# Product-key experts without gathers: every expert streamed through matmuls, half of the tokens at a time

## The chip, the cores and the metric

The kernel runs on one core of a Trainium2 chip. The metric is the device time of one execution in microseconds (us), as the median of several runs. Beside it stands a profiled execution, taken by the hardware profiler, in which every instruction has its start and its duration; all rows below come from that one execution of the kernel before. The engines are TensorE (PE, with its weight loads as PEld), VectorE (DVE), ScalarE (ACT), GpSimd (POOL) and the sync engine (SP), which here issues DMAs only. Sixteen DMA engines move the data between the HBM and the on-chip memory. Everything is float32.

## The reference

Two decoder layers over 512 tokens of 1024 numbers. Each layer is a mixer (retention, dilated attention and mLSTM heads over one input projection, then an output projection and a layer norm, giving x1), and then two things are added to x1: the PEER experts and a gated embedding.

```python
def peer(x, wq, sub_keys, expert_u, expert_v):          # T = 512 tokens, D = 1024
    qry = (xf @ wq).reshape(T, 8, 2, 128)               # 8 heads, two halves of a query
    sc = einsum('thpc,hpnc->thpn', qry, sub_keys)       # 128 keys in each half
    s1, i1 = top_k(sc[:, :, 0], 16); s2, i2 = top_k(sc[:, :, 1], 16)
    cand = s1[..., :, None] + s2[..., None, :]          # 16 x 16 sums a head
    cidx = i1[..., :, None] * 128 + i2[..., None, :]
    top_s, sel = top_k(cand, 16)                        # 16 experts of 16384 a head
    g = softmax(top_s)
    a = gelu(einsum('td,tkd->tk', xb, expert_u[ib]))    # 128 experts a token
    return einsum('tk,tkd->td', a * gb, expert_v[ib])

x1 = layer_norm(DN_ALPHA * x + mix, ln1_g, ln1_b)
e = sigmoid(x1 @ ple_wg + ple_bg) * (p @ ple_wp)
x = layer_norm(DN_ALPHA * x1 + y + e, ln2_g, ln2_b)
```

The expert matrices U and V are 16384 x 1024 each per layer, 64 MB each. A token needs 128 rows of each.

## The kernel before

The order of the work is written out by hand in one program for each engine; engines meet at semaphores. A list of steps (`MIXER_STEPS`, line 70) sets the order of TensorE in the mixer. Its last entries are the output projection in 8 steps of 16 TensorE instructions each (`out`, L1547), the transposes of x1, and the first queries and scores.

The tokens lie in four blocks of 128, one token to a partition. The unit of the expert stage is a pair n of a block and a head, 32 pairs a layer (`PAIRS`), 16 experts each. For each of these 16:

- GpSimd issues two gathers (`gather_u`, L558, and `gather_v`, L567). Each brings one row of 4 KB for each of the 128 tokens, by row numbers that VectorE has written in `rows`. There are 8 slots for U rows and 8 for V rows.
- VectorE multiplies the 128 U rows with the tokens and sums along the row (`dot_products`, L1066), one instruction of 128x1024.
- After 16 of them ScalarE applies gelu (L607), VectorE weighs the results with the softmaxed gates (L1091), and ScalarE writes 16 diagonal matrices with these weights (L795).
- TensorE multiplies each diagonal with the V rows of its expert, in two halves of 512 columns (L1610), and accumulates in two PSUM banks over the whole block. In the second half of the first block and at the end some V rows are added by VectorE instead (`add_row`, 32 rows a layer).

The selection of the experts for later pairs (top 16 of each half, of the 256 sums, and the row numbers; `halves_step` and `pairs_step`, L946 to L1055) is cut into small steps between the dot products of VectorE. Queries (`query`, L1416) and scores (`score`, L1431, L1437) for the first block run at the end of the mixer, and for the other three blocks during the first pairs, the gated embeddings (`embedding`, L1571 to L1575) in pairs 16 to 24. A block's second layer norm (`layer_norm`, L849 to L861) follows when its last rows are added. SP loads weights: w_in and w_out for the mixer, then for each head 1 MB of wq, and the embedding's weights in two halves.

In the mixer the lines that the prediction uses are: L842, VectorE's tensor_scalar of the head norms, with two scalars read from a column; L1209, the first tap of the convolution; L544, L548 and L551, GpSimd's products; L1389, the input projection (256 columns wide for `att_v`).

The inner loop of TensorE in the expert stage is this:

```python
for k in range(TOPK):
    e.wait_ge(v_in[i % VR], ...)
    if k % (2 * VD) == 0:
        e.wait_ge(diag_ready, tensor_rows(i + 2 * VD))
    for m in range(2):
        ins = e.matmul(bank[m][:, :], diag[:, k, :], vrow[i % VR][:, m * 512:(m + 1) * 512], ...)
    ins.then_inc(v_free, 1)
```

## Time and profile before

| what | value |
|---|---|
| median of 3 runs | 3440.74 us (3437.34 to 3442.32) |
| span of the profiled execution | 3781.1 us |
| TensorE busy | 3004.2 us, 79% |
| VectorE busy | 2120.8 us, 56% |
| GpSimd busy | 1984.4 us, 52% |
| ScalarE busy | 676.8 us, 18% |
| moved by DMA | 1174.41 MB, 311 GB/s over the span |
| of it gathers | 1073.87 MB |

The profiled execution is 9% longer than the median of the runs without a profiler. A matmul instruction's duration holds the time in which it runs through the array beside the next one, so the sum of durations says more than the engine's work; the distance between two starts (the pitch) is the price of one in a dense row of them.

### The profile page before, as it was taken

The page shows a single profiled execution, that of the slowest core. Times are in us where ns is not written, and L with a number is a line of the kernel's source. Part 1 is how long each engine was busy: PE and PEld are TensorE (multiplying, and loading weights), DVE is VectorE, ACT ScalarE, POOL GpSimd, SP SyncE. Part 2 cuts the span into 40 slices and gives each one's busy share as a digit, 9 for nine tenths or more (in the row PEclk, how much of TensorE's full clock was granted, in tenths as well). Part 3 has the DMA queues.
Part 4 walks back from the last instruction along what each step waited for, and adds up shares of the span by engine and source line. Part 5 has one row for each costly group of instructions (what it writes and reads, how often), then busy time and mean ns, then how long its engine had stood idle before and what let it go on. Part 6 is the DMA issues. An engine that isn't in the chain of part 4 may idle for free.

```text
span 3781.1 us, 25835 instructions
## 1 busy us (share of the span) xinstructions
PE 3004.2 (79%) x7696; PEld 1341.3 (35%) x7696; DVE 2120.8 (56%) x4948; ACT 676.8 (18%) x1658; POOL 1984.4 (52%) x2100
## 2 busy tenths in 40 slices
PE   8999777778778888777699987777777788887776
PEld 4555433333223323222245544333322233333222
DVE  1447665575555655665424476665656555656654
ACT  1331111111111112111013211111111111121110
POOL 0014455566665666666500145555566666666665
PEclk9999888889999999999999998888899999999999
DMA  4127899998999999999831278998899999989998
GB/s 153 67 70 256 313 342 344 346 350 338 399 368 351 355 384 355 348 371 367 336 129 67 70 269 316 353 347 339 335 363 407 363 352 363 385 329 362 371 370 321
DMA packets 360799, 1174.41 MB, mean 311 GB/s; under 512 B 36946, under 2 KB 75986, under 8 KB 360404
## 3 DMA queue, kind: packets, MB, share of 16 engines
q0 software_dynamic: 294912, 1073.87, 74.7%
q1 hardware_dynamic: 63284, 98.59, 7.6%
q8 instruction: 61, 1.00, 0.1%
q10 hardware_dynamic: 2464, 0.31, 0.1%
q14 instruction: 78, 0.64, 0.0%
HBM read 1170.54 MB, written 2.10 MB: 310 GB/s over the span
## 4 chain that ended last, share of the span: by engine, by line
PE 27%; DVE 18%; POOL 16%; issue 15%; another core or an unknown queue 11%; DMA 9%; ACT 4%; DVEq 1%; ACTq 0%; SPq 0%; POOLq 0%
DVE arena L1066 10%; POOL arena L567 9%; PE bank L1610 8%; POOL arena L558 8%; DMA arena<-in_peer_v,rows 5%; PE bank L1389 5%; DMA arena<-in_peer_u,rows 4%; PE yv L1389 3%; ACT arena L795 3%; PE bank L1416 2%; PE yv L1547 1%; PE bank L1437 1%; PE yv L1467 1%; PE bank L1547 1%
## 5 line engine op out<-in xcount | busy, mean ns | idle before, releaser
L1610 PE MATMUL bank<-arena 128*128 128x512 f32 x3840 | 1906.7, 637 | 523.0 <-DMA arena<-in_peer_v,rows 318.4
L1066 DVE CUSTOM_DVE_ANT_0 arena<-arena,xps 128x1024 f32<-128x1024 f32 x1024 | 1237.4, 1214 | 629.3 <-DMA arena<-in_peer_u,rows 464.2
L567 POOL DMA_INDIRECT arena<-in_peer_v,rows x1024 | 974.6, 952 | 714.1 <-issue 281.8
L1610 PEld LDWEIGHTS bank<-arena 128*128 128x128 f32 x3840 | 719.3, 200 | 1696.4 <-issue 938.4
L558 POOL DMA_INDIRECT arena<-in_peer_u,rows x1024 | 972.5, 950 | 552.1 <-issue 293.0
L607 ACT ACTIVATE arena<-arena 128x16 f32<-128x16 f32 x64 | 13.9, 218 | 1897.9 <-issue 1160.9
L795 ACT ACTIVATE arena<-keep,arena 128x128 f32<-128x128 f32 x960 | 294.2, 388 | 299.1 <-remote 147.8
L1416 PE MATMUL bank<-xT,arena 128*128 128x128 f32 (+1 forms) x1024 | 250.2, 399 | 57.4 <-issue 55.5
L1416 PEld LDWEIGHTS bank<-xT,arena 128*128 128x128 f32 x1024 | 165.3, 203 | 132.5 <-issue 72.3
L1389 PE MATMUL bank<-arena,xT 128*128 128x512 f32 (+1 forms) x448 | 187.1, 573 | 6.4 <-DMA arena<-in_w_in 4.3
L1389 PE MATMUL yv<-arena,xT 128*128 128x512 f32 (+1 forms) x320 | 132.6, 569 | 0.0
L1437 PE MATMUL bank<-arena 128*128 128x128 f32 x192 | 46.9, 434 | 100.5 <-ACTq L628 90.8
L1339 DVE TENSOR_TENSOR arena<-arena,bank 128x512 f32<-128x512 f32 x16 | 11.0, 687 | 195.3 <-ACTq L806 118.1
L1389 PEld LDWEIGHTS bank<-arena,xT 128*128 128x128 f32 x448 | 84.9, 193 | 99.8 <-issue 90.7
L1571 PE MATMUL bank<-arena,xT 128*128 128x512 f32 x256 | 112.5, 592 | 0.0
L544 POOL TENSOR_TENSOR arena<-arena,normg 128x256 f32<-128x256 f32 x8 | 5.8, 726 | 189.7 <-ACTq L719 189.7
L1437 PEld LDWEIGHTS bank<-arena 128*128 128x128 f32 x192 | 42.2, 329 | 119.2 <-ACTq L628 106.0
L1066 DVE DVE_READ_ACCUMULATOR2_ANT arena<- 128x1 f32 x1024 | 84.1, 82 | 0.0
L1389 PEld LDWEIGHTS yv<-arena,xT 128*128 128x128 f32 x320 | 60.9, 195 | 62.1 <-issue 60.5
L540 POOL MEMSET arena<- 128x3 f32 x8 | 0.4, 101 | 142.5 <-PE xps L1485 142.5
L1571 PEld LDWEIGHTS bank<-arena,xT 128*128 128x128 f32 x256 | 48.6, 190 | 61.2 <-issue 61.2
L1547 PE MATMUL yv<-arena,xT 128*128 128x512 f32 x160 | 69.7, 592 | 0.0
(288 smaller groups left out, 1966.1 us busy)
## 6 DMA issues: line engine op xcount, KB each, us to landing
arena<-in_peer_wq SPq DMA_DIRECT2D x32, 1024.0 KB
arena<-in_w_in SPq DMA_DIRECT2D x12, 2048.0 KB, 8.0
arena<-in_peer_u,rows POOLq DMA_INDIRECT x1024
arena<-in_peer_v,rows POOLq DMA_INDIRECT x1024
arena<-in_w_out SPq DMA_DIRECT2D x4, 2048.0 KB, 8.2
arena<-in_ple_wg SPq DMA_DIRECT2D x4, 2048.0 KB
arena<-in_mixer SPq DMA_DIRECT2D x2, 2112.0 KB, 19.4
ln<-in_ln SPq DMA_DIRECT2D x8, 512.0 KB, 7.9
```

The source lines that it names most:

```text
L558: e.indirect_dma_start(urow[i % UR], None, a["peer_u"], bass.IndirectOffsetOnAxis(ap=rows[:, n % RR, k:k + 1], axis=0)).then_inc(u_in[i % ...
L567: e.indirect_dma_start(vrow[i % VR], None, a["peer_v"], bass.IndirectOffsetOnAxis(ap=rows[:, n % RR, k:k + 1], axis=0)).then_inc(v_in[i % ...
L607: e.activation(act_d, dots[:, n % 2, :], ACT.Gelu).then_inc(gelu_done, 1)
L795: e.activation(diag[:, k, :], ident, ACT.Copy, scale=wgt[:, n % 2, k:k + 1]).then_inc(diag_ready, 1)
L1066: e.tensor_tensor_reduce(r, r, xps[:, :], 1.0, 0.0, ALU.mult, ALU.add, dots[:, n % 2, k:k + 1]).then_inc(u_free, 1)
L1389: ins = e.matmul(ps[:, 0:w], xT[:, k, i * P:(i + 1) * P], wt[:, k, :], start=(k == 0), stop=(k == KT - 1))
L1416: ins = e.matmul(ps[:, at:at + hi - lo], wq[m % 2][:, k, n * P:(n + 1) * P], xT[:, k, lo:hi], start=(k == 0), stop=(k == KT - 1))
L1437: ins = e.matmul(ps[:, b * NKEYS:(b + 1) * NKEYS], qT[:, s, b * P:(b + 1) * P], keys[m % KR][:, s, :], start=True, stop=True)
L1467: ins = e.matmul(ps[:, :], wt[:, k, i * P:(i + 1) * P], xT[:, k, :], start=(k == 0), stop=(k == KT - 1))
L1547: ins = e.matmul(ps[:, :], xT[:, k, b * P:(b + 1) * P], wt[:, k % 4, side * 512:(side + 1) * 512], start=(k == 0), stop=(k == KT - 1))
L1571: e.matmul(ps[:, :], xT[:, k, b * P:(b + 1) * P], wg[:, k, :], start=(k == 0), stop=False)
L1610: ins = e.matmul(bank[m][:, :], diag[:, k, :], vrow[i % VR][:, m * 512:(m + 1) * 512], start=(h == 0 and k == 0), stop=(h == PH - 1 and k ...
```

## The change

The gathers go. In their place each of the 16384 experts is applied to each token, and the gates, which are zero for all but the 128 chosen experts of a token, leave the others out.

- The tokens are taken in two passes of 256 (`PASSES`, `PB` = 2 blocks). In each pass 128 tiles of 128 experts are read in order, U and V, by SP.
- U tiles come in four DMAs, each into 32 partitions, laid so that VectorE's transpose of 32x32 blocks over 128x1024 (`turn`) leaves a quarter of the 1024 inputs in each group of 32 partitions. x1 is rearranged to the same order by GpSimd before its transposes, and wq and ple_wg are loaded in quarters.
- `dots`: 8 matmul calls of 256 columns for a tile give 128 experts x 256 tokens. ScalarE applies gelu (`gelu`), VectorE multiplies with the gates of the tile (`weigh`), and `mix_rows` multiplies with the V tile: 4 calls of 512 columns, accumulated in PSUM over the 128 tiles of the pass. TensorE does the dots of tile n + 2 before the rows of tile n.
- The gates of a pass are a map of 128 x 128 expert numbers x 256 tokens (`gate`). A token's map is one matmul of 128x128: a one-hot matrix of the second halves' numbers (128 choices x 128) times one of the first halves' with the gate as its value. The two are written by `make_hot`, on GpSimd for the first 40 tokens and every third, otherwise on VectorE, in a ring of 4 slots. ScalarE copies four maps at a time (`copy_gates`).
- The whole selection of the first two blocks is made before the first tile, that of the other two blocks in steps between the tiles of pass 0. The maps of the second pass are made between the passes.
- Queries of both halves and all gated embeddings come before the first tile. The sum of alpha times x1 and the embedding is built in `x` by GpSimd and kept in the HBM while `x` holds the scores of the second half.

The diff, cut to its core:

```diff
+TILES = EXPERTS // P
+PASSES = 2
+PB = NB // PASSES
+PT = PB * P
+RING = 3
+AHEAD = 2
+UR, TR, VR, QR = 2, 2, 3, 4
+GROUP = 4
+HOT = GROUP
+DQ, DP = 4, 32
...
-    + [("out", 0), ("out", 1), ("out", 2), ("x1_tr", 0), ("q", (0, 0)), ("s", (0, 0)), ("q", (1, 0)), ("s", (1, 0)),
-       ("out", 3), ("out", 4), ("out", 5), ("out", 6), ("out", 7),
-       ("q", (2, 0)), ("s", (2, 0)), ("q", (3, 0)), ("s", (3, 0))]
+    + [("out", 0), ("out", 1), ("out", 2), ("out", 3), ("x1_tr", 0), ("out", 4), ("out", 5), ("x1_tr", 1),
+       ("out", 6), ("out", 7), ("q", (0, 0)), ("q", (1, 0)), ("s", (0, 0)), ("x1_tr", 2), ("q", (2, 0)), ("s", (1, 0)),
+       ("q", (3, 0)), ("s", (2, 0)), ("x1_tr", 3), ("q", (4, 0)), ("s", (3, 0)), ("q", (5, 0)), ("s", (4, 0)),
+       ("q", (6, 0)), ("s", (5, 0)), ("q", (7, 0)), ("s", (6, 0)), ("s", (7, 0))]
...
+GATE_STEPS = (
+    [("ple", u) for u in range(2 * NB)]
+    + [("q", (0, 1)), ("q", (1, 1)), ("s", (0, 1)), ("q", (2, 1)), ("s", (1, 1)), ("exp", 0)]
+    + [t for h in range(3, PH) for t in (("q", (h, 1)), ("s", (h - 1, 1)))] + [("s", (PH - 1, 1)), ("sel", 0)]
+    + spreads(0, 0, 10) + [("exp", 1)] + spreads(0, 10, GROUPS_A_BLOCK) + [("sel", 1)] + spreads(1, 0, GROUPS_A_BLOCK)
+)
+NEXT_STEPS = [t for b in range(PB, NB) for t in [("sel", b)] + spreads(b, 0, GROUPS_A_BLOCK)]
...
+def on_pool(b, t):
+
+    return b == 0 and t < 40 or t % 3 == 2
...
+        def make_hot(e, b, t):
+
+            e.wait_ge(selT_ready, b + 1)
+            n = b * P + t
+            if n >= HOT:
+                e.wait_ge(*hot_consumed(*TOKENS[n - HOT]))
+            h = hot[:, n % HOT]
+            e.tensor_scalar(h[:, 1, :], iota, selT[:, 1, t:t + 1], None, ALU.is_equal)
+            e.tensor_scalar(h[:, 0, :], iota, selT[:, 0, t:t + 1], selT[:, 2, t:t + 1], ALU.is_equal, ALU.mult).then_inc(hot_made(b, t)[0], 1)
...
+                def load_u(n):
+                    if n >= UR:
+                        e.wait_ge(u_turned, n - UR + 1)
+                    at = (l * TILES + n % TILES) * P
+                    src = a["peer_u"][at:at + P, :].rearrange("(g e) (q d) -> q e g d", g=DQ, q=DQ)
+                    for q in range(DQ):
+                        dst = utile[n % UR][q * DP:(q + 1) * DP, :].rearrange("p (g d) -> p g d", g=DQ)
+                        e.dma_start(dst, src[q]).then_inc(u_in[n % UR], 16)
+                def load_v(n):
+                    if n >= VR:
+                        e.wait_ge(v_used, n - VR + 1)
+                    e.dma_start(vtile[n % VR], a["peer_v"][(l * TILES + n % TILES) * P:(l * TILES + n % TILES + 1) * P, :]).then_inc(v_in[n % VR], 16)
+                for n in range(PASSES * TILES):
...
+                    load_u(n + AHEAD + UR + 1)
+                    load_v(n + VR)
...
+                def copy_gates(b, n):
+                    t = (b % PB) * P + n * GROUP
+                    if b >= PB:
+                        e.wait_ge(w_ready, (b // PB) * TILES)
+                    src = work_read(e, "spread", (b, n)).rearrange("p (t e) -> p e t", t=GROUP)
+                    e.copy(gate[:, :, t:t + GROUP], src).then_inc(work_freed("spread", (b, n)), 1)
+                def gelu(n):
+                    e.wait_ge(dots_full, n + 1)
+                    if n >= RING:
+                        e.wait_ge(v_used, n - RING + 1)
+                    e.activation(ring[:, n % RING, :], bank[n % 2][:, 0:PT], ACT.Gelu).then_inc(gelu_done, 1)
...
+                def turn(n):
+                    if n < PASSES * TILES:
+                        e.wait_ge(u_in[n % UR], DQ * 16 * (n // UR + 1))
+                        if n >= TR:
+                            e.wait_ge(dots_full, n - TR + 1)
+                        e.transpose(turned[n % TR].rearrange("p k g e -> p g k e"), utile[n % UR].rearrange("p (g k c) -> p g k c", g=DQ, k=KT)).then_inc(u_turned, 1)
+                def weigh(n):
+                    p, j = divmod(n, TILES)
+                    if j == 0:
+                        e.wait_ge(gate_written, p + 1)
+                    e.wait_ge(gelu_done, n + 1)
+                    r = ring[:, n % RING, :]
+                    e.tensor_tensor(r, r, gate[:, j, :], ALU.mult).then_inc(w_ready, 1)
...
+                def spread(b, n):
+                    ps = work_fill(e, "spread", (b, n))
+                    for i in range(GROUP):
+                        t = n * GROUP + i
+                        e.wait_ge(*hot_made(b, t))
+                        h = hot[:, (b * P + t) % HOT]
+                        ins = e.matmul(ps[:, i * P:(i + 1) * P], h[:, 1, :], h[:, 0, :], start=True, stop=True)
+                        ins.then_inc(work_filled("spread", (b, n)) if i == GROUP - 1 else hot_used, 1)
+                def dots(n):
+                    p = n // TILES
+                    e.wait_ge(u_turned, n + 1)
+                    if n >= 2:
+                        e.wait_ge(gelu_done, n - 1)
+                    u = turned[n % TR].rearrange("p k g e -> p k (g e)")
+                    for k in range(KT):
+                        ins = e.matmul(bank[n % 2][:, 0:PT], u[:, k], xT[:, k, p * PT:(p + 1) * PT], start=(k == 0), stop=(k == KT - 1))
+                    ins.then_inc(dots_full, 1)
+                def mix_rows(n):
+                    p, j = divmod(n, TILES)
+                    e.wait_ge(v_in[n % VR], 16 * (n // VR + 1))
+                    e.wait_ge(w_ready, n + 1)
+                    for b in range(PB):
+                        for m in range(2):
+                            ins = e.matmul((yv, xps)[b][:, m * 512:(m + 1) * 512], ring[:, n % RING, b * P:(b + 1) * P], vtile[n % VR][:, m * 512:(m + 1) * 512], start=(j == 0), stop=(j == TILES - 1))
+                    ins.then_inc(v_used, 1)
...
+                for n in range(AHEAD):
+                    dots(n)
+                for n in range(PASSES * TILES):
+                    if n == TILES:
+                        for step, i in NEXT_STEPS:
...
+                    if n + AHEAD < PASSES * TILES:
+                        dots(n + AHEAD)
+                    mix_rows(n)
```

## Rows read from the trace of the kernel before

**Rows 1.** The page: span, busy time, the gathers' queue (packets, MB, share).

```profile
span 3781.1 us, 25835 instructions
PE 3004.2 (79%) x7696; PEld 1341.3 (35%) x7696; DVE 2120.8 (56%) x4948; ACT 676.8 (18%) x1658; POOL 1984.4 (52%) x2100
q0 software_dynamic: 294912, 1073.87, 74.7%
```

**Rows 2.** Windows: stretch, its length, busy us of each engine, clock, DMA share, GB/s.

```profile
1500.00:1800.00 300.00, 220.54 (x449) 82.24 (x448) 182.89 (x398) 54.80 (x143) 199.09 (x208) 0.95 0.95 359
```

**Rows 3.** Timeline of TensorE at 1200 us: start, length, instruction, idle before and releaser.

```profile
1201.85 1.98 PE L1610 MATMUL bank<-arena 128*128 128x512 f32 x4 [0.58 <-DMA arena<-in_peer_v,rows]
1204.41 1.98 PE L1610 MATMUL bank<-arena 128*128 128x512 f32 x4 [0.58 <-DMA arena<-in_peer_v,rows]
```

**Rows 4.** Groups of instructions by line: busy us, mean ns, idle before.

```profile
L1610 PE MATMUL bank<-arena 128*128 128x512 f32 x3840 | 1906.7, 637 | 523.0 <-DMA arena<-in_peer_v,rows 318.4 <-issue 134.7 <-ACT arena L795 59.2
```

**Rows 5.** Timeline of TensorE, dense stretches of 256, 128 and 512 columns.

```profile
134.47 3.62 PE L1389 MATMUL bank<-arena,xT 128*128 128x256 f32 x16
304.89 3.74 PE L1416 MATMUL bank<-xT,arena 128*128 128x128 f32 x32
309.73 13.90 PE L1547 MATMUL yv<-arena,xT 128*128 128x512 f32 x32
323.46 13.90 PE L1547 MATMUL bank<-arena,xT 128*128 128x512 f32 x32
```

**Rows 6.** Windows as in the second group, and a piece of the chain (start, length).

```profile
353.00:358.00 5.00, 4.81 (x33) 4.62 (x31) 3.20 (x6) 1.96 (x4) 4.09 (x4) 0.75 1.05 386
362.00:391.60 29.60, 29.41 (x66) 13.03 (x67) 25.38 (x67) 5.84 (x16) 15.18 (x15) 0.94 0.94 345
362.19 29.40 PE bank L1610 x64
```

**Rows 7.** Timeline, one line's durations (min/median/max ns), GpSimd's groups.

```profile
134.50 4.19 DVE L842 TENSOR_SCALAR acc<-acc,mv,rstd 128x128 f32<-128x128 f32 x16
L842 DVE TENSOR_SCALAR acc<-acc,mv,rstd x64: 302/336/1276, 134.5 to 2151.9; 128x128 f32<-128x128 f32 x32, 128x64 f32<-128x64 f32 x32
269.32 1.32 POOL L548 TENSOR_TENSOR arena<-arena,normg 128x512 f32<-128x512 f32 x1 [8.66 <-ACTq L730]
270.79 1.26 POOL L551 TENSOR_TENSOR acc<-acc,arena 128x512 f32<-128x512 f32 x1
L544 POOL TENSOR_TENSOR arena<-arena,normg 128x256 f32<-128x256 f32 x8 | 5.8, 726 | 189.7 <-ACTq L719 189.7
```

**Rows 8.** Groups that price VectorE's and ScalarE's new work: busy us, mean ns.

```profile
L1209 DVE TENSOR_SCALAR arena<-arena,convw 128x512 f32<-128x512 f32 x8 | 3.9, 486 | 27.6 <-ACTq L698 27.6
L1143 DVE TENSOR_TENSOR arena<-bank,arena 128x256 f32<-128x256 f32 x12 | 4.5, 414 | 0.0
L987 DVE FIND_INDEX8 topi<-arena 128x8 uint32<-128x128 f32 x28 | 8.0, 285 | 0.0
L1026 DVE FIND_INDEX8 pos<-arena 128x8 uint32<-128x256 f32 x28 | 11.7, 419 | 0.0
L1040 DVE TENSOR_TENSOR arena<-arena,keep 128x1024 f32<-128x1024 f32 x28 | 34.4, 1227 | 3.2 <-remote 2.2
L778 ACT COPY xT<-bank 128x512 f32<-128x512 f32 x12 | 7.0, 586 | 2.8 <-PE bank L1584 2.7
```

**Rows 9.** Timeline and chain: first out step, end of layer 0, output.

```profile
277.60 7.03 PE L1547 MATMUL bank<-arena,xT 128*128 128x512 f32 x16
1884.30 1.28 DVE L1327 TENSOR_TENSOR acc<-acc,bank 128x512 f32<-128x512 f32 x2
1890.79 9.05 DMA arena<-in_w_in
2165.94 13.73 PE yv L1547 x32
3774.14 0.39 SPq L520 DMA_DIRECT2D out<-x  x1
```

927 lines of the change are left out of this document (354 added, 573 removed).

## The prediction

> **What bounds the kernel now.** I read the page first: TensorE is busy 79% of the span, and the software queue of the gathers moves 1073.87 MB and takes 74.7% of the 16 DMA engines' time over the span, mixers included [rows 1]. A busy share names no bound, so I took one late window and the timeline inside the gather stage. In 1500 to 1800 us the DMA engines are 95% busy at 359 GB/s, TensorE 220.54 of 300 us, VectorE 182.89 [rows 2]. The timeline shows four TensorE instructions of 1.98 us and then 0.58 us of waiting for a V row set, again and again, every 2.56 us [rows 3]. One such turn moves one U and one V row per token, 2 x 128 x 4 KB = 1.05 MB. So the expert stage goes at the pace of the gathers (512 turns a layer); it lasts from 362 to 1884 us in the first layer [rows 6, 9], 2.97 us a turn on average, and TensorE, VectorE and GpSimd stand below it. The mixers are TensorE work and don't change.
>
> **The unit of the new work.** Line 1610 is called 1920 times (512 turns a layer less 32 on VectorE, two halves, two layers) and shows 3840 instructions [rows 4]: a float32 matmul call is two instructions. In dense stretches at the full clock their pitch is: 512 columns, 32 in 323.46 - 309.73 = 13.73, so 0.429 us; 256 columns, 16 in 3.62 - 0.17 (what the length holds over the starts, 13.90 - 13.73), so 0.2156 us; 128 columns, (3.74 - 0.17)/32 = 0.112, of which I take 0.116 [rows 5]. Their weight loads lie beside them. The pitch is two cycles a column at 2.4 GHz, so a call costs four.
>
> **The tile loop (added).** Each pass takes 128 tiles of 128 experts, for 256 tokens. A tile is 8 calls over 256 columns (dots) and 4 over 512 (mix_rows): 16 x 0.2156 + 8 x 0.429 = 6.88 us; I keep 6.89. Two passes and two layers are 512 tiles: 3530 us, more than the whole median of before. The bytes fall to half, 512 tiles x 1.05 MB = 537 MB instead of 1074, but they no longer set the time. What lies beside it: per tile 1.05 MB in 6.89 us is 152 GB/s, against 345 and 359 GB/s in rows of before [rows 2, 6]. No row has a load into 32 partitions as the four quarters of a U tile are; if it ran like any other, 1.05 MB take 3.0 us; a quarter of the rate for the U half would be 1.5 + 6.1 = 7.6 us and show. I take it as hidden, since the loads are issued two to three tiles ahead. The Trainium skill, "SBUF — State Buffer", section "Door 1: The DMA port swizzle", says that 32 partitions reach 8 of 16 ports, about half the rate; by that a tile's loads would take some 4.2 us (an estimate from that page), still under the tile, and no row here shows it. VectorE per tile: one 128x1024 block transpose, for which there is no row (bounds: twice the 128x512 tensor_scalar, 0.97 us, and a 128x1024 tensor_tensor, 1.23; I take 1.2, since nothing says that a transpose has the tensor_scalar's pace), a 128x256 product 0.41, and in pass 0 a selection step of 1.1 us with 8 in 7 tiles [rows 8]: 2.9 us. ScalarE: a 128x256 activation, under the 0.59 of a 128x512 copy [rows 8]. Dots run two tiles ahead of rows, so the transpose has ten us of slack behind its last wait, and gelu and weighing seven. A wait whose semaphore is there costs TensorE nothing: 64 instructions of line 1610 with a wait every fourth took 29.40 us, 27.5 of pitch and 1.9 at a clock of 0.94, which is worth 1.8 [rows 6]. So 6.89 us stand, with a bound of 7.3 for stalls I don't see.
>
> **The one-hot stage (added), the least certain term.** For each token two VectorE or GpSimd operations of 128x128 write a one-hot and a weighted one-hot, one call (two instructions of 128 columns, 0.23 us [rows 5]; where the clock stood at 0.75, 33 of them took 4.81 us, 0.146 each [rows 6], so at the half clock some 0.47 a call) makes the token's 128x128 gate map, and ScalarE copies four of them (0.59 us for 128x512, 0.15 a token [rows 8]). Four slots are shared. 256 tokens are made before pass 0, 256 between the passes, with TensorE's queue standing in front of the next dots, so nothing of the tile loop covers it. VectorE's tensor_scalar with pointer scalars takes (4.19 - 0.34)/15 = 0.257 us for 128x128 [rows 7]. GpSimd has only tensor_tensor rows: 1.26 us for 128x512, 0.726 for 128x256, which gives 0.45 for 128x128, and 0.14 between two [rows 7]; a one-input form may be cheaper, a pointer may cost more, so 0.35 to 0.7. If both engines ran side by side a token would cost 0.51 x 2/3 plus waits, 0.42 us. They don't: of 64 instructions of line 842 with a median of 0.34 us one took 1.28, the one that met a GpSimd tensor_tensor of 1.32 us [rows 7]. Serial, three tokens are 4 x 0.257 + 2 x 0.45 = 1.93 us, 0.64 a token; with handovers I take 0.72. The Trainium skill, the same page, section "SBUF: two separate sides", calls this an exclusive lock of the port pair which both share, and the trace agrees (1.28 against 0.34). The first 40 tokens of pass 0 are GpSimd's alone: 2 x 0.45 + 2 x 0.14 = 1.2 us each, 47 us. So 47 + 216 x 0.72 = 203 us in pass 0 and 256 x 0.72 = 184 in pass 1: 387 us a layer. Ends: 246 (0.42 a token) and 47 + 472 x 1.0 = 520 (half clock and handovers in a row).
>
> **The rest of a layer.** From the first out step: 8 x 6.87 = 55; four blocks of 8 transposes 4; the queries of 256 tokens, 8 heads x 32 x 0.2156 = 55, and scores, 8 x 8 x 0.116 = 7.5; waits 3: 125 us (rearranging x1 on GpSimd, some 2.5 us a block, lies behind the next out step). Embeddings, moved ahead of the experts, 8 x 22 x 0.429 + 2 = 77; they were done under gathers before and are now TensorE time. Their GpSimd part is 3 x 1.27 us per 9.4, hidden. Queries and scores of the second half 63 + 3 for the wait on the copy of x to HBM: 66. Selection of half 0 on VectorE: per pair of heads 20 operations of 0.28, 10 of 0.415, three of 1.22, small ones 1.7 and 16 drains of some 0.15: 17.5 us, eight pairs 140 [rows 8]. It can begin 82 us after the first out step and TensorE has work until 268, so it is hidden with 46 us to spare. Four turnovers of selT at 3 us: 12. Fill of the two tile loops 8. End of layer, two adds and two norms at 6.5 us a block [rows 9]: 13.
> Per layer 125 + 77 + 66 + 12 + 387 + 2 x 128 x 6.89 (1765) + 8 + 13 = 2453 us.
>
> **Sum.** The mixer ends at 277.6 us in layer 0 and takes 2159.1 - 1890.8 = 268.3 in layer 1 (2159.1 is the yv group's 2165.94 less one out step of 6.87), the output 7.0 [rows 9]. 277.6 + 268.3 + 7 + 2 x 2453 = 5459 us of profiled span, against 3781.1. The median of before, 3440.7, is 9% under its own profiled span. Dense TensorE stretches sit at the pitch of the clock in the profile, so they can't shrink by that; 3530 us are tile loops, and of the other 1930 us I take 1% off. The forecast is 5440 us, 58% more than the 3440.7.
>
> **Rivals.**
> (a) GpSimd and VectorE don't wait for each other on the one-hots, or their forms are cheap: 0.42 us a token, 2 x 141 us less, 5160. For: the operation is another (a comparison). Against: it reads one tensor and column scalars, as the one that waited. 0.15.
> (b) The one-hot chain is slower, 1.0 us a token: four slots, each held over make, semaphore, matmul at half clock and semaphore. 2 x 133 us more, 5705. For: TensorE would be under half busy there, and a window with short gaps shows 0.75 of the clock [rows 6]. Against: 0.72 x 4 = 2.9 us a slot leaves room. 0.15.
> (c) The tile loop isn't TensorE's: U quarters at a quarter of the rate, 7.6 us a tile, 512 x 0.7 more, 5800. Against: twofold slack over any rate seen. 0.08.
> (d) The other side. Streaming wins if a float32 column costs one cycle in these calls and not four: dots and rows 1.72 us a tile, the loop then at the loads' 3.0 us; 5440 - 512 x 3.9 = 3443, and the queries and embeddings, 188 us a layer, fall by 141: 3160, 8% faster. It decides where (5440 - 282 - 3441)/512 = 3.35 us are gone from a tile, at 3.5 us a tile. Against: every dense row has four cycles a column [rows 5]. 0.01.
> That it doesn't do what it says is hardly open: the order is written out in each engine's program, and the number of calls is fixed.
>
> **Chances.** Forecast 0.61 with its own range of 5300 to 5600; (a) 0.15, (b) 0.15, (c) 0.08, (d) 0.01. The range must reach (a) and (b): 5150 to 5760. Faster by over 0.2% has 0.01 (case d), within 0.2% (about what a measurement here can tell from no change) 0.00, slower 0.99.
>
> **What would show it.** TensorE near 100% busy in the tile loop with pitch 0.216 and 0.429, a tile every 6.9 us, clock 1.0, DMA share some 0.4, no wait on u_in or v_in. Between the loops two stretches a layer of 180 to 200 us, in which VectorE and GpSimd operations of the one-hots stretch each other and TensorE is a third busy. Selection of the first half done before TensorE reaches the first sel step. I would be wrong if a tile took more than 7.3 us, if a token cost under 0.5 or over 0.95 us, or if TensorE waited between the embeddings and the one-hots.

## The result, and the profile after

The changed kernel takes 5235.86 us (median of 4 runs, 5234.65 to 5238.57), 1.522 times the 3439.04 us of the kernel before on the same chip (interval 1.520 to 1.525). The forecast was 5440 us with an own range of 5300 to 5600 and a range of 5150 to 5760: the sign and the size are right, the time lies 204 us under the forecast and below the forecast's own range. The page of the changed kernel, where [rows 1] showed TensorE at 79% and the gathers' queue at 74.7%:

```profile
span 5232.6 us, 51117 instructions
PE 4952.3 (95%) x18216; PEld 3267.7 (62%) x18216; DVE 1882.0 (36%) x4854; ACT 593.5 (11%) x1180; POOL 677.8 (13%) x888
...
POOL 0002840000007200000000028300000071000000
PEclk9999799999999999999999997999999999999999
...
PE 87%; POOL 8%; issue 3%; DVE 1%; DMA 0%; DVEq 0%; ACT 0%; ACTq 0%; SPq 0%; POOLq 0%
```

TensorE is now busy 95% of the span and 87% of the chain that ended last. GpSimd works only in four short stretches, and there it is the rest of the chain, 8%. Three windows with their columns as in [rows 2]: the two one-hot stages of layer 0, and the middle of its first tile loop:

```profile
545.00:700.00 155.00, 95.59 (x478) 72.22 (x479) 79.90 (x282) 35.12 (x61) 149.38 (x210) 0.80 0.06 18
1601.00:1728.00 127.00, 86.02 (x516) 70.28 (x517) 92.56 (x341) 37.25 (x64) 121.04 (x166) 0.95 0.00 1
1000.00:1500.00 500.00, 500.00 (x1743) 331.66 (x1742) 180.05 (x433) 33.71 (x79) 0.00 (x0) 1.00 0.60 153
```

In the tile loop TensorE is busy 500.00 of 500 us at the full clock, and the DMA engines carry 153 GB/s, not the 359 of [rows 2]. In the one-hot stages it is GpSimd that is full: 149.38 of 155 us and 121.04 of 127, TensorE 62 and 68%. The groups that stand for the priced work (busy us, mean ns, idle before and who ended it):

```profile
L1443 PE MATMUL bank<-xT,arena 128*128 128x256 f32 x8192 | 1851.5, 379 | 1.3 <-DVE arena L951 1.3
...
L951 DVE STREAM_TRANSPOSE arena<-arena 128x1024 f32<-128x1024 f32 x512 | 637.2, 1245 | 2430.2 <-PE bank L1443 2397.5
...
L1455 PE MATMUL yv<-arena 128*128 128x512 f32 x2048 | 962.6, 593 | 0.0
...
L1432 PE MATMUL bank<-arena 128*128 128x128 f32 x2048 | 375.8, 320 | 217.8 <-POOL arena L455 200.1
...
L454 POOL TENSOR_SCALAR arena<-keep,arena 128x128 f32<-128x128 f32 x390 | 243.5, 624 | 1927.2 <-ACTq L644 1911.4
...
L455 POOL TENSOR_SCALAR arena<-keep,arena 128x128 f32<-128x128 f32 x390 | 329.9, 846 | 0.0
L454 DVE TENSOR_SCALAR arena<-keep,arena 128x128 f32<-128x128 f32 x634 | 199.2, 314 | 123.7 <-PE bank L1432 116.3
L455 DVE TENSOR_SCALAR arena<-keep,arena 128x128 f32<-128x128 f32 x634 | 235.6, 372 | 0.2
```

The dots (L1443) waited 1.3 us in the whole run, the mix (L1455) nothing. The one wait that counts is that of the gate maps (L1432) for GpSimd's second operation, 200.1 us. The 512 map instructions of each stage, in the windows from the first to the last of them (only that line's work is counted):

```profile
543.84:708.00 164.16, 101.26 (x512) 76.63 (x512) 0.81 0.06 17
1600.87:1728.04 127.17, 85.85 (x512) 69.98 (x512) 0.95 0.00 1
3153.84:3319.11 165.27, 103.84 (x512) 78.91 (x512) 0.79 0.06 17
4211.97:4338.62 126.65, 84.81 (x512) 68.87 (x512) 0.96 0.02 4
```

So the span divides into 543.84 us up to the first map, 164.2 + 127.2 for the one-hots of layer 0, 892.9 and 874.6 for its tile loops (1600.87 - 708.00, and 1728.04 to the last mix instruction at 2602.6), 551.2 from there to the first map of layer 1, the same four pieces again (165.3, 892.9, 126.6, 874.6), and 19.4 for the end.

How the one-hot stage runs is seen in the timeline of pass 0 at 642 us (start, length, instruction, idle before and releaser):

```profile
641.91 0.60 POOL L454 TENSOR_SCALAR arena<-keep,arena 128x128 f32<-128x128 f32 x1
641.97 0.75 PEld L1432 LDWEIGHTS bank<-arena 128*128 128x128 f32 x6 [0.77 <-POOL arena L455]
641.98 0.94 PE L1432 MATMUL bank<-arena 128*128 128x128 f32 x6 [0.58 <-POOL arena L455]
642.49 0.79 POOL L455 TENSOR_SCALAR arena<-keep,arena 128x128 f32<-128x128 f32 x1
642.58 0.43 DVE L454 TENSOR_SCALAR arena<-keep,arena 128x128 f32<-128x128 f32 x1 [0.54 <-PE bank L1432]
...
642.93 0.43 DVE L455 TENSOR_SCALAR arena<-keep,arena 128x128 f32<-128x128 f32 x1
643.19 0.27 DVE L454 TENSOR_SCALAR arena<-keep,arena 128x128 f32<-128x128 f32 x1
```

GpSimd makes every third token, one after the other with no gap: 0.60 and 0.79 us, and the next begins. VectorE's operations run beside it, at 0.43 instead of 0.27 us where they are stretched most, and VectorE waits 0.54 us for a slot. TensorE takes three tokens (six instructions) each time that GpSimd's is ready. GpSimd is stretched too, in other turns:

```profile
1639.85 0.92 POOL L455 TENSOR_SCALAR arena<-keep,arena 128x128 f32<-128x128 f32 x1
```

That is 0.92 us against 0.79, and the mean of its second operation beside VectorE's is 0.86. So two of GpSimd's instructions take some 1.48 us, and a third of that is the 0.49 us a token of the steady stage. The two engines delay each other by up to some 0.16 us an instruction, and neither is shut out for the whole of the other's instruction; GpSimd is the slowest.

### The profile page after: what moved, and what is told of

Read it like the earlier page. It is cut to its first block, busy times and chain, and to the rows that moved or that the text cites. A ratio compares the mean times of both kernels' runs of the same rounds, so it can differ in the third digit from the quotient of the medians.

```text
span 5232.6 us, 51117 instructions
## 1 busy us (share of the span) xinstructions
PE 4952.3 (95%) x18216; PEld 3267.7 (62%) x18216; DVE 1882.0 (36%) x4854; ACT 593.5 (11%) x1180; POOL 677.8 (13%) x888
## 3 DMA queue, kind: packets, MB, share of 16 engines
q8 instruction: 148, 2.42, 0.2%
## 4 chain that ended last, share of the span: by engine, by line
PE 87%; POOL 8%; issue 3%; DVE 1%; DMA 0%; DVEq 0%; ACT 0%; ACTq 0%; SPq 0%; POOLq 0%
PE bank L1443 34%; PE xps L1455 17%; PE yv L1455 17%; POOL arena L454 4%; PE bank L1268 4%; POOL arena L455 3%; PE bank L1244 3%; PE yv L1244 3%; PE bank L1409 2%; PE yv L1389 1%; PE bank L1389 1%; PE yv L1309 1%; PE bank L1413 1%; PE bank L1279 1%; PE bank L1432 1%
## 5 line engine op out<-in xcount | busy, mean ns | idle before, releaser
L1443 PE MATMUL bank<-xT,arena 128*128 128x256 f32 x8192 | 1851.5, 379 | 1.3 <-DVE arena L951 1.3
L1443 PEld LDWEIGHTS bank<-xT,arena 128*128 128x128 f32 x8192 | 1559.8, 190 | 424.6 <-issue 240.6
L951 DVE STREAM_TRANSPOSE arena<-arena 128x1024 f32<-128x1024 f32 x512 | 637.2, 1245 | 2430.2 <-PE bank L1443 2397.5
L1455 PE MATMUL xps<-arena 128*128 128x512 f32 x2048 | 962.6, 593 | 0.0
L1455 PE MATMUL yv<-arena 128*128 128x512 f32 x2048 | 962.6, 593 | 0.0
L1455 PEld LDWEIGHTS xps<-arena 128*128 128x128 f32 x2048 | 390.1, 190 | 488.7 <-issue 488.7
L1432 PE MATMUL bank<-arena 128*128 128x128 f32 x2048 | 375.8, 320 | 217.8 <-POOL arena L455 200.1
L1455 PEld LDWEIGHTS yv<-arena 128*128 128x128 f32 x2048 | 390.1, 190 | 272.2 <-issue 246.4
L454 POOL TENSOR_SCALAR arena<-keep,arena 128x128 f32<-128x128 f32 x390 | 243.5, 624 | 1927.2 <-ACTq L644 1911.4
L1432 PEld LDWEIGHTS bank<-arena 128*128 128x128 f32 x2048 | 294.5, 209 | 299.5 <-POOL arena L455 199.2
L455 POOL TENSOR_SCALAR arena<-keep,arena 128x128 f32<-128x128 f32 x390 | 329.9, 846 | 0.0
L454 DVE TENSOR_SCALAR arena<-keep,arena 128x128 f32<-128x128 f32 x634 | 199.2, 314 | 123.7 <-PE bank L1432 116.3
L455 DVE TENSOR_SCALAR arena<-keep,arena 128x128 f32<-128x128 f32 x634 | 235.6, 372 | 0.2
L1268 PE MATMUL bank<-xT,arena 128*128 128x256 f32 x1024 | 227.1, 381 | 0.0
L1268 PEld LDWEIGHTS bank<-xT,arena 128*128 128x128 f32 x1024 | 193.0, 190 | 28.3 <-issue 1.9
```

What stands on the lines that cost most here:

```text
L454: e.tensor_scalar(h[:, 1, :], iota, selT[:, 1, t:t + 1], None, ALU.is_equal)
L455: e.tensor_scalar(h[:, 0, :], iota, selT[:, 0, t:t + 1], selT[:, 2, t:t + 1], ALU.is_equal, ALU.mult).then_inc(hot_made(b, t)[0], 1)
L951: e.transpose(turned[n % TR].rearrange("p k g e -> p g k e"), utile[n % UR].rearrange("p (g k c) -> p g k c", g=DQ, k=KT)).then_inc(u_turn ...
L1268: ins = e.matmul(ps[:, n * PT:(n + 1) * PT], wq[m % QR][:, k, n * P:(n + 1) * P], xT[:, k, g * PT:(g + 1) * PT], start=(k == 0), stop=(k = ...
L1432: ins = e.matmul(ps[:, i * P:(i + 1) * P], h[:, 1, :], h[:, 0, :], start=True, stop=True)
L1443: ins = e.matmul(bank[n % 2][:, 0:PT], u[:, k], xT[:, k, p * PT:(p + 1) * PT], start=(k == 0), stop=(k == KT - 1))
```

## The experiments

All edits are to the changed kernel. Four of the runs were executed once (another operation on VectorE, the tensor_tensor, the U tile in one piece, the loads by groups); the executions of each of the others lie within 0.8% of each other. The first group asks what the one-hot stage costs and why, the second whether the tile loop could have been anything else.

**GpSimd's first share made small.**

```diff
-    return b == 0 and t < 40 or t % 3 == 2
+    return b == 0 and t < 8 or t % 3 == 2
-    + spreads(0, 0, 10) + [("exp", 1)] + spreads(0, 10, GROUPS_A_BLOCK) + ...
+    + spreads(0, 0, 2) + [("exp", 1)] + spreads(0, 2, GROUPS_A_BLOCK) + ...
```

> GpSimd alone makes only the first 8 tokens of pass 0 instead of 40 (its gates' exp is moved up accordingly); from then on every third is GpSimd's, as before. Theory S (the two engines work side by side, and GpSimd's own 1.44 us for each of its tokens sets the pace, 0.49 us a token when it has every third): 32 tokens fall from 1.44 to 0.49 us in each layer, 61 us in all, 5175 us. Rival W (VectorE is still selecting for the second block when the one-hots begin, so the 40 tokens cover it): no more than 20 us are gained, 5215 us or more.

Measured: 5178.79 us, 57 us less; the two first stages fell from 164 and 165 us to 136 and 137, the other two stayed at 127. The 32 tokens taken from GpSimd gave back 28.5 us a layer, so each cost 0.89 us more than the common rate of 0.49: 1.38 us. And VectorE, which was still at the selection of the second block when the stage began, could have taken its share much earlier: in the changed kernel its part of that selection pauses at 551.2 us, and it then stands idle for 48.6 us, until ScalarE's exp for that block, which comes behind the first 40 tokens (the second line of the edit moves it up).

**Nearly all one-hots on VectorE.**

```diff
-    return b == 0 and t < 40 or t % 3 == 2
+    return b == 0 and t < 4
```

> All one-hots but the first 4 tokens of a layer on VectorE. Theory S: VectorE's two operations have a pitch of 0.22 and 0.26 us, so a token costs 0.48 and the stages become 127 us (164 in the changed kernel) and 123 (127); 41 us less a layer, 5154 us. Rival R (the ring of four slots sets the pace: make, semaphore, matmul, semaphore): a token stays near 0.6 us, 158 and 154 us, 5278 us or no gain.

Measured: 5137.09 us, 1.493 times the kernel before (1.489 to 1.497). The stages take 124.9, 117.7, 125.0 and 117.6 us, 0.46 us a token: with these instructions one engine alone is faster than the two together. Two tokens of its timeline at 640 us:

```profile
640.06 0.28 DVE L454 TENSOR_SCALAR arena<-keep,arena 128x128 f32<-128x128 f32 x1
...
640.25 0.34 DVE L455 TENSOR_SCALAR arena<-keep,arena 128x128 f32<-128x128 f32 x1
640.51 0.28 DVE L454 TENSOR_SCALAR arena<-keep,arena 128x128 f32<-128x128 f32 x1
```

From one L454 to the next are 0.45 us: an instruction begins before the one ahead of it has ended, so a token costs less than the 0.28 + 0.34 of its two.

**Another operation on VectorE.** The gates come out wrong, since VectorE subtracts and multiplies instead of comparing; the size and the operands are the same.

```diff
-            e.tensor_scalar(h[:, 1, :], iota, selT[:, 1, t:t + 1], None, ALU.is_equal)
+            e.tensor_scalar(h[:, 1, :], iota, selT[:, 1, t:t + 1], None, ALU.is_equal if on_pool(b, t) else ALU.subtract)
```

(and the comparison of the next line likewise)

> VectorE's two one-hot operations do a subtraction (and a product) in place of the comparison, as line 842 of the kernel before does; the gates are wrong thereby, nothing else changes. If VectorE's kind of operation decides whether it waits for GpSimd (as my prediction took it from that line), its longest operations rise from 0.45 to 0.9 us and a token costs 0.64 us or more, 5300 us. If GpSimd's form decides (a tensor_tensor there, a tensor_scalar here), durations and time stay as they are, 5236 us.

Measured: 5240.46 us, with stages of 165.0, 127.0, 165.7 and 127.5 us, as in the changed kernel. Minimum, median and maximum in ns of VectorE's first and second operation:

```profile
L454 DVE TENSOR_SCALAR arena<-keep,arena x634: 271/286/442, 604.4 to 4343.3; 128x128 f32<-128x128 f32 x159
...
L455 DVE TENSOR_SCALAR arena<-keep,arena x634: 329/343/460, 604.6 to 4343.5; 128x128 f32<-128x128 f32 x159
```

Nothing like the 1.28 us of [rows 7]. That the operation is a comparison doesn't explain why VectorE isn't held.

**A tensor_tensor on GpSimd.** What stood beside the long VectorE operation in [rows 7] was a tensor_tensor. Here GpSimd's first one-hot operation is one (a subtraction, so the gates come out wrong).

```diff
+            if on_pool(b, t):
+                e.tensor_tensor(h[:, 1, :], iota, selT[:, 1, t:t + 1].to_broadcast([P, P]), ALU.subtract)
+            else:
                 e.tensor_scalar(h[:, 1, :], iota, selT[:, 1, t:t + 1], None, ALU.is_equal)
```

> The changed kernel, but GpSimd's first operation of a one-hot is a tensor_tensor (a subtraction, so the gates are wrong) that reads two tensors, in place of a tensor_scalar. Theory G (GpSimd's reading of two tensors holds VectorE off, which is what line 842 of the kernel before met): VectorE's one-hot operations that meet it stretch to 0.5 us and more, maximum over 0.6 in place of 0.44. GpSimd's operation itself takes some 0.45 us in place of 0.60, so that its token costs 1.3 us and the time falls 0 to 30 us, or rises where VectorE's waits outweigh it. If maxima stay under 0.45, the wait at line 842 had another cause.

Measured: 5157.06 us. The durations of GpSimd's tensor_tensor and of VectorE's first operation:

```profile
L455 POOL TENSOR_TENSOR arena<-keep,arena x390: 393/434/1291, 542.9 to 4258.8; 128x128 f32<-128x128 f32 x195
...
L457 DVE TENSOR_SCALAR arena<-keep,arena x634: 270/285/497, 593.1 to 4260.0; 128x128 f32<-128x128 f32 x159
```

VectorE's longest is 0.50 us. But it is held: its second operation has a median of 0.42 us here, against 0.34 in the changed kernel, and in 248 cases begins in the last 0.3 to 0.37 us of GpSimd's tensor_tensor and ends 0.08 us after it. That hold can't be long because this instruction isn't.

So line 842 is no single case, and the kept traces show what decides. In the changed kernel it comes back in the mixer (L827 is line 842 of the kernel before) and in the selection, beside GpSimd's tensor_tensor of 128x512:

```profile
412.14 1.53 POOL L601 TENSOR_TENSOR x<-x,arena 128x512 f32<-128x512 f32 x1
412.47 1.25 DVE L893 CAST arena<-topi 128x64 f32<-128x64 uint32 x1
...
L827 DVE TENSOR_SCALAR arena<-arena,mv,rstd x64: 302/336/1290, 135.4 to 2879.8; 128x128 f32<-128x128 f32 x32, 128x64 f32<-128x64 f32 x32
```

A cast whose median is 0.19 us takes 1.25 and ends 0.05 us after GpSimd's instruction. Thirty VectorE instructions of this trace begin inside such a tensor_tensor, with over 0.25 us of it to come, and are short enough to end before it does. Thirteen of them last beyond its end: casts, copies, tensor_scalars and products with all operands in the on-chip memory SBUF. The other 17, which read PSUM or are steps of the top-16 search, keep their usual length.

The one-hot operations themselves are held too. In the bfloat16 runs below VectorE makes all of them, and the first of GpSimd's casts of a V tile fall into that stage:

```profile
559.02 1.04 POOL L618 CAST arena<-arena 128x1024 bf16<-128x1024 f32 x1 [76.25 <-DMA arena<-in_peer_v]
559.09 1.05 DVE L467 TENSOR_SCALAR arena<-keep,arena 128x128 f32<-128x128 f32 x1
...
L467 DVE TENSOR_SCALAR arena<-keep,arena x1024: 327/335/1216, 552.8 to 3347.3; 128x128 f32<-128x128 f32 x171
```

In the six bfloat16 runs 25 one-hot operations of VectorE begin in the first 0.6 us of such a cast; each takes 0.5 to 1.2 us and ends 0.08 us after the cast. So VectorE's operation is of the kind that is held, and how long is set by what GpSimd runs. Beside GpSimd's one-hot tensor_scalars the hold is short: in the changed kernel the VectorE operations that they stretch end 0.08 us behind GpSimd's or 0.16 to 0.28 us before its end, and none is over 0.46 us. Why GpSimd's tensor_scalar lets VectorE in before it has ended stays open.

The run also shows that GpSimd's tensor_tensor is its cheaper form, a median of 0.43 us against 0.60 for the tensor_scalar, and since GpSimd sets the pace, that took 79 us off, where I had expected 30 at most. The stages of pass 1 take 109.0 and 109.6 us, 0.43 us a token, less than the 117.7 and 117.6 of VectorE alone. So in the steady stage the help pays with this form and costs with the other.

**A smaller steady share for GpSimd.** Every fourth and every fifth token instead of every third.

```diff
-    return b == 0 and t < 40 or t % 3 == 2
+    return b == 0 and t < 8 or t % 4 == 3
```

> As the run with 8 tokens on GpSimd alone, and then every fourth token on GpSimd instead of every third. Theory S: four tokens take the longer of GpSimd's 1.44 and VectorE's 3 x 0.48 us, so 0.36 to 0.40 a token; pass 0 about 107 us (164), pass 1 about 97 (127), 5062 us. Rival L (the operations do slow each other when they overlap, 0.28 to 0.40 us as single rows show): 0.45 a token, 5110 us. Rival R (slots): no gain over every third, 5175.

```diff
-    return b == 0 and t < 40 or t % 3 == 2
+    return b == 0 and t < 8 or t % 5 == 4
```

> GpSimd alone makes the first 8 tokens, then every fifth, whose place moves through the four slots (every fourth token is always the same slot, and its making can't begin before its last matmul is done). Theory A (that alignment made every fourth slow): five tokens take 4 x 0.46 us of VectorE, over GpSimd's 1.44, 0.37 us a token; pass 0 about 105 us, pass 1 about 95, 5050 us. Rival N (GpSimd's share is a loss in any pattern, since its late tokens hold up the order): 0.45 us a token or more, not under the 5137 us of VectorE alone.

Measured: 5279.86 and 5229.64 us. Theories S and A missed by 218 and 180 us; of all that was expected only rival N of the second run holds (0.54 us a token, not under 5137). With every fourth token the stages take 161, 152, 161 and 153 us: less work for the slow engine, and more time. Its timeline at 641 us:

```profile
640.65 0.60 POOL L454 TENSOR_SCALAR arena<-keep,arena 128x128 f32<-128x128 f32 x1 [0.72 <-PE bank L1432]
...
641.23 0.96 POOL L455 TENSOR_SCALAR arena<-keep,arena 128x128 f32<-128x128 f32 x1
...
642.25 2.07 PE L1432 MATMUL bank<-arena 128*128 128x128 f32 x8 [1.10 <-POOL arena L455]
...
643.22 0.60 POOL L454 TENSOR_SCALAR arena<-keep,arena 128x128 f32<-128x128 f32 x1 [1.02 <-PE bank L1432]
```

There are four slots, taken in turn. With every fourth token GpSimd always gets the same slot and can't begin (it waits 1.02 us) until TensorE has read its last token, while TensorE waits 1.10 us for the new one. The two take turns, some 2.4 us for four tokens, 0.6 us each. With every third, GpSimd's next slot is another one, and free; it works without a gap and the rate is its 1.4 to 1.5 us by three. With every fifth the period is 2.5 us for five in this stretch, and GpSimd waits 0.94 us in each; over a stage it is 0.54 us a token. The order says why moving the slot didn't help: token n may be made when token n - 4 has been read. With every third token GpSimd's next one needs the one before its own last, with every fourth its own last, with every fifth the one behind that. So a ring of four slots in token order runs at the slow maker's round trip as soon as that maker's stride is four or more. A longer ring, which by this account would free it, wasn't tried.

**The tile loop in bfloat16.** This asks for the rival on the other side: what bounds the loop once a column costs one cycle and a call one instruction? ScalarE casts each transposed U tile, GpSimd each V tile, and the one-hots are all on VectorE. The experts' products have bfloat16's precision.

```diff
+    e.copy(ub[n % 3], turned[n % TR]...).then_inc(u_cast, 1)            # ScalarE
+    e.tensor_copy(vb[n % 2], vtile[n % VR]).then_inc(v_cast, 1)         # GpSimd
-    ins = e.matmul(bank[n % 2][:, 0:PT], u[:, k], xT[:, k, p * PT:(p + 1) * PT], ...)
+    ins = e.matmul(bank[n % 2][:, 0:PT], u[:, k, :], xTb[:, k, p * PT:(p + 1) * PT], ...)
-    ins = e.matmul(..., ring[:, n % RING, b * P:(b + 1) * P], vtile[n % VR][:, m * 512:(m + 1) * 512], ...)
+    ins = e.matmul(..., ringb[n % RING][:, b * P:(b + 1) * P], vb[n % 2][:, m * 512:(m + 1) * 512], ...)
```

> The tile loop in bfloat16, on top of the run with the one-hots on VectorE (here all of them): ScalarE casts the transposed U tile, GpSimd the V tile, the gates and the weights are kept as bfloat16; queries, scores and embeddings stay float32. Theory C (the four cycles a column and nothing else set the tile's 6.89 us): a call is one instruction with a pitch of 0.107 to 0.12 us (256 columns) and 0.214 (512), 1.8 us of TensorE a tile, and the next limit shows: GpSimd's cast of 128x1024 (2 x 1.26 us by the 128x512 rows of before, 2.5), VectorE 2.9 in pass 0, loads 3.0 at the gathers' rate. So 3.0 to 3.3 us a tile and 5137 - 512 x 3.7 = 3240 us, faster than the kernel before. Rival D (loads into 32 partitions go at half the rate, and that bounds a tile; the Trainium skill, SBUF — State Buffer, Door 1: The DMA port swizzle, gives about 4.2 us a tile by estimate): 4.2 us a tile, 3760 us, slower than before. Rival F (something else holds the tile, such as a wait in the chain transpose, cast, dots, gelu, weigh): over 4.5 us, over 3900 us.

Measured: 3954.12 us, 1.150 times the kernel before (1.141 to 1.159); theory C's 3240 us missed, and rival D had the right limit with 3760. The dots of 256 columns now follow each other by 0.109 us where they are dense, half of the 0.2156 of one float32 instruction and a quarter of a call: one cycle a column. A window in pass 0 and one in pass 1:

```profile
700.00:1000.00 300.00, 169.73 (x786) 85.60 (x801) 184.62 (x398) 91.35 (x137) 70.36 (x66) 0.78 0.98 233
1450.00:1600.00 150.00, 83.30 (x383) 40.76 (x388) 73.22 (x72) 45.75 (x68) 33.29 (x32) 0.80 1.00 230
```

The DMA engines are 98 to 100% busy, and yet they bring 230 to 233 GB/s where the gathers brought 359 [rows 2]. A tile takes 4.5 us in both passes (578.6 and 573.8 us for 128). The loads bind, at two thirds of the rate that I had taken for them.

**The U tile in one piece.** The dots come out wrong, because a tile loaded so isn't in the layout that they need.

```diff
-                    for q in range(DQ):
-                        dst = utile[n % UR][q * DP:(q + 1) * DP, :].rearrange("p (g d) -> p g d", g=DQ)
-                        e.dma_start(dst, src[q]).then_inc(u_in[n % UR], 16)
+                    e.dma_start(utile[n % UR], a["peer_u"][at:at + P, :]).then_inc(u_in[n % UR], DQ * 16)
```

> As the bfloat16 run, but a U tile comes in one DMA over all 128 partitions, one row of 4 KB to a partition, in place of four into 32 partitions with pieces of 1 KB; the dots are wrong thereby. If loads bound the bfloat16 tile (rival D there), a tile falls to 3.0 us and 512 times the difference is gained, up to 600 us. If not, the time stays within 1% of that run.

Measured: 3527.51 us. The same two windows:

```profile
700.00:1000.00 300.00, 171.14 (x792) 84.92 (x807) 192.74 (x401) 93.32 (x139) 70.50 (x68) 0.80 0.67 235
1450.00:1600.00 150.00, 94.26 (x589) 55.09 (x600) 79.31 (x100) 67.23 (x102) 52.05 (x50) 1.00 0.97 352
```

Pass 1 now runs at 352 GB/s, 3.1 us a tile; the quartered load was its bound. In pass 0 the DMA engines are 67% busy and a tile still takes 4.3 us, with no engine over 64%. Its timeline showed a ring: VectorE's transpose 1.25 us, ScalarE's cast 1.04, its activation 0.38, VectorE's weighing 0.42 and a selection step, each waiting for the one ahead.

**All partitions at once, in the right layout.** Four DMAs by group of 32 experts, each into all 128 partitions; then the same with ScalarE's cast one tile less far ahead, to open the ring.

```diff
-                    src = a["peer_u"][at:at + P, :].rearrange("(g e) (q d) -> q e g d", g=DQ, q=DQ)
-                    for q in range(DQ): ...
+                    for g in range(DQ):
+                        src = a["peer_u"][at + g * DP:at + (g + 1) * DP, :].rearrange("e (q d) -> q e d", q=DQ)
+                        dst = utile[n % UR][:, g * DQ * 64:(g + 1) * DQ * 64]
+                        e.dma_start(dst, src).then_inc(u_in[n % UR], 16)
```

> As e5_bf16 (tile loop in bfloat16, one-hots on VectorE), all of the computation done, but a U tile is loaded in four DMAs by group of 32 experts, each into all 128 partitions in pieces of 1 KB, instead of four DMAs by quarter of a row, each into 32 partitions, also in pieces of 1 KB. Theory P (the 32 partitions of each transfer hold the rate down): the loop runs as with the whole-tile load, 554 and 391 us instead of 578 and 569 us a layer, so about 3530 us. Theory Q (the 1 KB pieces hold it down, the 4 KB rows of the whole-tile load freed it): no change from 3954 us. In between (3700) if both do.

```diff
-                for n in range(AHEAD + 1):
+                for n in range(AHEAD):
                     cast_u(n)
...
-                    cast_u(n + AHEAD + 1)
+                    cast_u(n + AHEAD)
```

> As the kernel with four all-partition U loads, and ScalarE's cast of a U tile runs one tile less far ahead, so that it no longer waits for the transpose that VectorE puts behind the weighing of the same turn. In the whole-tile run a turn of pass 0 was a ring in a row: transpose 1.25, cast 1.04, activation 0.38, weighing 0.42 and a selection step of 0.8 to 1.2, together 4.3 us, though no engine had more than 3 us of work. Theory R (that ring sets pass 0): pass 0 falls from 4.3 to VectorE's own 3.0 to 3.3 us a tile, 2 x 128 x 1.1 = 280 us less than the kernel without it: 3250 us if theory P holds, faster than the kernel before by some 5%. Rival (pass 0 is bound by the selection on VectorE itself with its stretched operations): 3530 us. If theory Q holds, 3950 us for both.

Measured: 5410.18 and 5403.74 us, far outside every expectation. A window of the first of them, and SyncE's timeline:

```profile
700.00:1200.00 500.00, 230.32 (x789) 107.26 (x804) 175.07 (x406) 91.99 (x137) 69.81 (x67) 0.61 0.46 141
...
904.06 4.91 SPq L537 DMA_DIRECT2D arena<-in_peer_u  x4
909.02 2.30 SPq L545 DMA_DIRECT2D arena<-in_peer_v  x1
911.36 5.21 SPq L537 DMA_DIRECT2D arena<-in_peer_u  x4
```

The DMA engines are 46% busy while SyncE sits in its own issues, some 1.3 us for one of U instead of 0.43. The packet records of 900 to 915 us show three to six pieces of U in flight, against 13 to 18 while a quarter comes in in the run before that had quarters. The source's first dimension has four entries here and 32 there. The Trainium skill, "DMA: Bandwidth & Descriptors", section "Why a DMA increments its semaphore by 16 and not by 1", has the rule: a transfer is spread over as many of the 16 engines, at most, as divide the slowest dimension of both sides, so four here. The trace agrees, with some four pieces in flight. I hadn't looked it up before I wrote the edit, and neither run tested what it was made for.

**Two queues.** Quarters 0 and 1 from SyncE, 2 and 3 from ScalarE behind its cast of the tile two before, and the cast less far ahead.

```diff
-                    for q in range(DQ):                                  # SyncE
+                    for q in range(DQ // 2):
+                        for q in range(DQ // 2, DQ):                     # ScalarE
+                            dst = utile[n % UR][q * DP:(q + 1) * DP, :].rearrange("p (g d) -> p g d", g=DQ)
+                            e.dma_start(dst, src[q]).then_inc(u_in[n % UR], 16)
```

> As e5_bf16 with its quartered U loads, all of the computation done, and two edits: quarters 0 and 1 of a U tile are issued by SyncE as before, quarters 2 and 3 by ScalarE behind its cast, so that pieces for different partitions are in flight together; and ScalarE's cast runs one tile less far ahead. The trace of the kernel with group loads showed that run to be no test of the partitions: only four DMA engines worked on its U pieces at a time, at 47 ns a piece of 1 KB, against 72 ns in e5 with sixteen. Theory P (pieces that go to the same 32 partitions hold each other up): a turn of pass 1 falls from 4.5 us to 3.1 to 3.4, the piece to some 50 to 55 ns, and pass 0 to VectorE's 3.0 to 3.4: 3954 - 4 x 128 x 1.2 = 3340 us at most, 3240 at best, faster than the kernel before by 3 to 6%. Theory Q (the size of the piece or its reading from HBM, whichever partitions it goes to): both passes stay at 4.4 us a tile, 3940 us, the piece at 70 ns or over. If pass 1 falls and pass 0 stays at 4.3 us, P is right and the ring of transpose, cast, activation and weighing isn't what binds pass 0.

Measured: 3804.84 us, 1.106 times the kernel before (1.104 to 1.108), the fastest with nothing of the computation left out. The window of pass 1:

```profile
1450.00:1600.00 150.00, 90.66 (x432) 44.78 (x430) 54.88 (x71) 46.98 (x71) 36.72 (x35) 0.81 1.08 249
```

249 GB/s instead of 230, 4.2 us a tile instead of 4.5, and a piece of 1 KB still takes 73 to 76 ns in the packet records. Pieces for different quarters side by side take 6% off a tile, not the third that was missing; the DMA engines are full in this window, so the moved cast has no visible part in it. The Trainium skill, "SBUF — State Buffer", section "Can I just issue two DMAs to hit both halves?", says just that, with a gain of 6% too: only one transfer that spans all partitions reaches all ports.

**Pieces of 1 KB into all partitions.** The dots come out wrong as with the tile in one piece. Pass 0 loads U whole; pass 1 loads it in four DMAs of 128 partitions by 1 KB, from a source whose first dimension has 128 entries. The cast is less far ahead.

```diff
+                    if n < TILES:
+                        e.dma_start(utile[n % UR], a["peer_u"][at:at + P, :]).then_inc(u_in[n % UR], DQ * 16)
+                        return
+                    for g in range(DQ):
+                        dst = utile[n % UR][:, g * DQ * 64:(g + 1) * DQ * 64]
+                        e.dma_start(dst, a["peer_u"][at:at + P, g * DQ * 64:(g + 1) * DQ * 64]).then_inc(u_in[n % UR], 16)
```

> The dots are left wrong: a U tile isn't brought into the layout that they need. Otherwise as the bfloat16 loop with ScalarE's cast one tile less far ahead. In pass 0 a U tile comes in one DMA of 4 KB rows, as in e7; in pass 1 in four DMAs of 128 partitions by 1 KB, all sixteen DMA engines at work on each. Two questions, one by pass. Pass 0, where e7 had 554 us: theory R (the ring of transpose, cast, activation and weighing with a selection step) 390 to 430 us; its rival (VectorE's own work) 540 to 554. Pass 1, where the whole-tile load had 391 us and the quarters of 32 partitions 569: theory P (the 32 partitions) 391 to 410, a piece under 55 ns; theory Q (the piece of 1 KB, wherever it goes) 530 to 570, a piece over 65 ns. Sums from e7's 3527: R and P 3240, R and Q 3590, P alone 3530, Q alone 3870 us.

Measured: 3312.96 us, 0.963 times the kernel before (0.960 to 0.966). The windows of pass 0 and pass 1:

```profile
700.00:1000.00 300.00, 192.03 (x1138) 109.11 (x1161) 269.87 (x586) 131.77 (x197) 104.56 (x97) 0.97 0.92 338
1450.00:1600.00 150.00, 90.92 (x519) 50.69 (x528) 67.96 (x89) 58.47 (x88) 47.26 (x44) 0.94 0.93 309
```

Pass 0 takes 398.8 us instead of 555.2: the ring was its bound, and moving one instruction by one turn opened it (VectorE is now 90% busy, the DMA engines 92%). Pass 1 takes 436.2 us, 3.4 a tile, at 309 GB/s, against 352 for rows of 4 KB and 230 for the quarters; in the packet records a 1 KB piece takes 46 ns here and 72 in the quarters. So of what the quarters lose, the smaller pieces are the lesser part (352 to 309) and their place, 32 partitions with four pieces in a row in each, the greater (309 to 230). Whether it is the number of partitions or the several pieces in one of them, no run separates. A kernel that is faster than the one before with all of its work done wasn't reached: it would need this rate in the layout that the dots want.

## Why the prediction was right or wrong

Forecast against measured on the profiled executions, 5459 and 5232.6 us, in the order of the steps:

- **Unit and tile loop: right.** A tile takes 6.887 us (median from one tile's first dot to the next) against 6.89. Two cycles a column, twice, read off three dense stretches [rows 5], held for all 12,288 instructions of the loop. The waits that the bound of 7.3 allowed for weren't there.
- **Its cover: right, but thinner than I had thought.** No load bound the loop at 6.9 us. Yet the twofold slack by which rival (c) had its 0.08 wasn't there: the loads alone take 4.5 us a tile (bfloat16 run), not 3.0. The estimate that stood beside it, from the Trainium skill's "SBUF — State Buffer", section "Door 1: The DMA port swizzle", was 4.2 us and the nearer number. The prediction tried a quarter of the rate for the U half and not a half of it, which by its own rows is 1.5 + 3.0 = 4.5 us, as measured.
- **VectorE's transpose:** 1.245 us, taken at 1.2 and just above its bounds of 0.97 and 1.23; the weighing 0.38 against 0.41.
- **One-hot stage: the step that failed.** 387 us a layer forecast, 291.4 and 291.9 measured, 190.7 too many in all. The sentence is "They don't": I took the 1.28 us at line 842 for a lock over the whole of any instruction of the other engine, and made a token the serial sum of 0.64 us and handovers. (It was two instructions of the 64 and not one, 128x64, of 1.27 and 1.28 us, in either layer beside the same GpSimd instruction.) The hold is real, but beside GpSimd's one-hot operations it is some 0.16 us at most and not the whole of their 0.60 and 0.79 us. So the one-hots do run side by side, at 0.49 us a token in the steady stage, just under the 0.5 that the prediction had named as a sign of being wrong. I also had GpSimd's operation at 0.45, where its two take 0.60 and 0.79, the second above my upper bound of 0.7. The two errors worked against each other: with side by side alone I would have had rival (a), 0.42 us and 5160; with the true prices in a serial sum, 4 x 0.257 + 1.39 = 2.42 us for three, 0.81. The Trainium skill's "SBUF — State Buffer", section "SBUF: two separate sides", ties the lock on VectorE's side to an operation in a two-port mode or with two tensors read, and has it last for the whole instruction; I had taken it for the one-hots without asking which of their forms it means. The traces agree with a hold of the whole instruction beside GpSimd's wide ones: a VectorE one-hot operation of 0.34 us took 1.05 beside a cast of 1.04. They don't where GpSimd runs the one-hot tensor_scalars: there none took over 0.46 us, and the measurement decides.
- **The first 40 tokens:** 1.38 us each against 1.2, so 55 us instead of 47; the other 216 take (164.2 - 55)/216 = 0.51 us.
- **Rest of a layer.** From the mixer's end at 277.6 [rows 9] to the first map are 266 us, against the 268 of the three terms. Turnovers and fills were 20 us a layer, and the two tile loops with theirs take 1767.5 us against 1765 for the tiles alone. That makes most of another 36 us.
- **The 46 us to spare:** not there. The selection of the second block was still running at 549 us, when the first maps were being made. It cost little, since GpSimd alone was to make those tokens.
- **Span and median:** I took 1% of the rest off for the profiler, 19 us, and nothing was to be taken: 5232.6 against 5235.86 us. The 9% between the two in the kernel before have gone with its gathers.

-190.7 - 36 + 19 + 3 are the 204 us. The forecast had the right mechanism for the tiles and the wrong one for the one-hots; the range held because it reached to rival (a), and that the forecast lies only 204 us off is in part the luck of two errors that worked against each other. Of rival (d) the runs show a part: with one cycle a column the loop does fall to the loads, but to 4.5 us a tile and not to 3.0, and that is over the 3.5 us at which it would have been decided. So the change is slower for two reasons, one behind the other: four cycles a column, and behind them the quartered load.
